# A two-direction state-space scan and the z projection beside it, issued in fixed rounds

## The reference, cut to what matters

```python
def ssd_chunked(xs, dt, a, bm, cm):            # one direction
    a_cs = jnp.cumsum(adt, axis=-1)
    decay_in = jnp.exp(jnp.where(tri, seg, -jnp.inf))        # 128 x 128 per chunk and head
    cb = jnp.einsum("bclgn,bcsgn->bcgls", cc, bc)            # 128 x 128 per chunk and group
    y_diag = jnp.einsum("bcgls,bcgrls,bcsgrp->bclgrp", cb, decay_in, xd)
    states = jnp.einsum("bclgn,bcgrl,bclgrp->bcgrpn", bc, decay_states, xd)
    h = h * dec + state                                      # over the chunks, in order
    y_off = jnp.einsum("bclgn,bcgrpn,bcgrl->bclgrp", cc, prev, jnp.exp(a_cs))
...
    y = y_fwd + y_bwd + d_skip * xs
    return rms_norm(y * jax.nn.silu(z), ssd_norm)            # z = h @ w_in[:, 768:1792]
```

## Time and profile before

| | |
|---|---|
| median of 3 runs | 2354.16 us (2347.55, 2354.16, 2356.76) |
| profiled execution | 2345.79 us, of which 2344.0 us are its span |
| PE busy | 2198.4 us, 94% |
| DVE, ACT, POOL busy | 1142.7, 1004.5, 962.0 us |
| granted PE clock, mean over the span | 0.961 |

### The profile page before, as it was taken

One profiled execution on the slowest core, in us unless ns is written; L12 is line 12 of the kernel. 1 busy time (PEld: TensorE's weight loads), 2 busy tenths in 40 slices (PEclk: granted clock), 3 DMA queues, 4 the chain that ended last, 5 costly groups with the idle time before them and its releaser, 6 DMA issues.

```text
span 2344.0 us, 28202 instructions
## 1 busy us (share of the span) xinstructions
PE 2198.4 (94%) x10837; PEld 1826.0 (78%) x10848; DVE 1142.7 (49%) x1836; ACT 1004.5 (43%) x2027; POOL 962.0 (41%) x730
## 2 busy tenths in 40 slices
PE   7999899999988997899999998998899999999997
PEld 5788778888877776778888877785697887888886
DVE  3445565554344666465554363664445335544322
ACT  5666444443235555244443254655243234323222
POOL 3655553433457652444333442224323334322232
PEclk9999999999999999799999997998899999999998
DMA  4111122232213221122222221110012232222221
GB/s 157 55 55 60 49 99 99 90 108 99 94 60 102 82 68 39 62 82 90 98 100 97 88 88 36 37 36 19 19 46 101 88 108 72 92 106 90 101 99 52
DMA packets 29846, 183.08 MB, mean 78 GB/s; under 512 B 3984, under 2 KB 4112, under 8 KB 11920
## 3 DMA queue, kind: packets, MB, share of 16 engines
q1 hardware_dynamic: 29712, 181.27, 22.4%
HBM read 174.97 MB, written 2.10 MB: 76 GB/s over the span
## 4 chain that ended last, share of the span: by engine, by line
PE 82%; DVE 6%; ACT 5%; issue 3%; POOL 2%; DMA 1%; SPq 0%; POOLq 0%; ACTq 0%; DVEq 0%
PE PS L1452 81%; PE PS L1577 1%; POOL LO L2735 1%; DVE bQS L2191 1%; PE PS L1690 0%; ACT HI L1779 0%; DMA RAW<-wall 0%; DVE aQS L2191 0%; DVE T_f L2263 0%; DVE XL L2268 0%; DVE YH L2293 0%; PE PS L1625 0%; POOL cQ L2818 0%; ACT bP L1995 0%; POOL cROT L2810 0%
## 5 line engine op out<-in xcount | busy, mean ns | idle before, releaser
L2735 POOL TENSOR_TENSOR LO<-RAW,HI 128x512 fp32r<-128x512 f32 (+2 forms) x382 | 540.9, 1432 | 601.6 <-ACT HI L1779 601.3
L1452 PE MATMUL PS<-XH,HI 128*128 128x512 f32 (+1 forms) x1584 | 637.6, 403 | 24.5 <-DVE XL L2191 6.7
L1452 PE MATMUL PS<-XH,LO 128*128 128x512 f32 (+1 forms) x1584 | 624.4, 394 | 0.0
L1452 PE MATMUL PS<-XL,HI 128*128 128x512 f32 (+1 forms) x1584 | 618.1, 395 | 1.0 <-DVE XL L2268 1.0
L1779 ACT ACTIVATE HI<-RAW 128x512 fp32r<-128x512 f32 (+3 forms) x668 | 365.4, 608 | 171.3 <-PE PS L1452 168.0
L2191 DVE TENSOR_TENSOR LO<-RAW,HI 128x512 fp32r<-128x512 f32 (+2 forms) x286 | 305.0, 1071 | 246.2 <-ACT HI L1779 245.8
L1452 PEld LDWEIGHTS PS<-XH,HI 128*128 128x128 f32 (+1 forms) x1584 | 302.2, 191 | 87.7 <-issue 20.4
L1452 PEld LDWEIGHTS PS<-XH,LO 128*128 128x128 f32 (+1 forms) x1584 | 301.4, 190 | 65.7 <-issue 0.8
L1452 PEld LDWEIGHTS PS<-XL,HI 128*128 128x128 f32 (+1 forms) x1584 | 300.8, 190 | 62.7 <-DVE XL L2268 2.5
L1452 PE MATMUL PS<-HH,HI 128*128 128x512 f32 x528 | 205.4, 389 | 0.0
L1452 PE MATMUL PS<-HL,HI 128*128 128x512 f32 x528 | 205.4, 389 | 0.0
(11 more groups left out here) (395 smaller groups left out, 3358.3 us busy)
## 6 DMA issues: line engine op xcount, KB each, us to landing
RAW<-wall SPq DMA_DIRECT2D x138, 1024.0 KB, 4.8
RAW<-wall SPq DMA_DIRECT2D x24, 896.0 KB, 4.4
bROT<-bTQ SPq DMA_DIRECT2D x64, 64.0 KB, 2.0
RAW<-wall SPq DMA_DIRECT2D x5, 512.0 KB, 3.3
XF<-xT SPq DMA_DIRECT2D x4, 512.0 KB, 5.2
outT<-XR SPq DMA_DIRECT2D x8, 256.0 KB, 2.0
FP<-cfp SPq DMA_DIRECT2D x1, 1024.0 KB, 6.7
MKF<-cmask SPq DMA_DIRECT2D x1, 704.0 KB, 10.8
```

What stands on the lines that cost most here:

```text
L1452: return e.matmul(out, a, b, start=start, stop=stop)
L2735: return e.tensor_tensor(out, x, h.bitcast(F32), ALU.subtract)
```

## The change

- The z units start right after the two CB products, and the generator `scan()` runs beside them at 1.12 steps per tick. It works in rounds: round r puts the exponent products of head r, the state product of item r-1, the state reading of item r-3, and y of head r-1, in that order on PE; `STATES` lists the state items, alternating directions. From round 2 on it waits until the last convolution is turned.
- Steps are split so that issue and completion stand apart: `se` (the exponentials), `sz` (the addition to Y), `sq` (scaling a reading and adding it), `sv` (taking a state in), `sd` (decaying the old state).
- The states alternate between two places (PRV and the new tiles PR2), so decaying doesn't wait for the reading.
- `em`: DVE adds the backward half of EM to the forward half and multiplies the sum with CB once. POOL has no part in it. `sy` has 4 products in place of 8, and there is one pair of banks for the exponents in place of two.
- z's gates go to tiles of their own (SZ, two units deep). Multiplying them into Y is a step `czm` of its own, put when the four heads of a group and all six state readings of its half are in Y. Unit i >= 2 waits for the `czm` of unit i-2.

```diff
-RATES = (0.37, 0.18, 1.12, 0.36, 1.0, 0.9, 0.9)
+STATES = ((0, 0, 0), (1, 0, 0), (0, 0, 1), (0, 1, 0), (1, 1, 0), (1, 0, 1), (0, 2, 0), (1, 2, 0), (0, 1, 1), (1, 1, 1), None,
+          (0, 2, 1), (1, 2, 1))
+RATES = (0.37, 0.18, 1.12, 1.12, 1.0, 0.9, 0.9)
...
+            while sdone[0] < 16 or sum(added) < 12:
+                while r >= 2 and ("cxt", CONV[-1]) not in steps:
                     yield
+                if 0 < r < 17:
+                    put("em", r - 1)
+                if item(r):
+                    put("sw", *item(r))
+                    if item(r)[1]:
+                        put("sd", *item(r))
+                if r < 16:
                     for dr in range(2):
+                        at_bank(("sh", r, dr), 2 + dr)
+                    put("sh", r)
                     yield
+                if item(r - 2):
+                    s = put("sv", *item(r - 2))
...
+                if item(r - 4):
+                    dr, idx, g = item(r - 4)
+                    freed[6] = ("sod", put("sq", dr, idx + 1, g))
+                    added[g] += 1
+                if item(r - 1):
+                    s = ("sp",) + item(r - 1)
+                    at_bank(s, 4 + s[1])
+                    put(*s)
                     yield
+                if r < 16:
+                    s = put("se", r)
...
+                if item(r - 3):
+                    dr, idx, g = item(r - 3)
+                    at_bank(put("so", dr, idx + 1, g), 6)
+                    yield
+                if 1 < r < 18:
+                    freed[7] = ("syd", put("sz", r - 2))
+                    sdone[0] = r - 1
+                if 0 < r < 17:
+                    at_bank(put("sy", r - 1), 7)
+                    yield
+                times()
...
-        first = opening()
-        while chores or together_chores:
-            chore()
-            next(first, None)
-        for _ in first:
-            pass
-        alongside(scans(), RATES[3])
-        until(lambda: sdone[0] >= 4 and all(finished))
+        alongside(scan(), RATES[3])
         for i in range(4):
             def evac(c, t):
-                if c == 0:
-                    until(lambda: sdone[0] >= 4 * i + 4)
-                return ("czd", put("cze", i, c, t))
+                if i >= 2:
+                    until(lambda: (i - 2, c) in timed)
+                s = put("cze", i, c, t)
+                gated.append((i, c))
+                times()
+                return "czd", s
...
                 for c in range(4):
-                    for dr in range(2):
-                        u = 1024 * (h % 2) + 512 * dr + 128 * c
-                        x = 1024 * c + 64 * h
-                        m = mm(PS[bank][:, 64 * c:64 * c + 64], EM[:, u:u + 128], XS[:, x:x + 64], dr == 0, dr == 1)
+                    u, x = 1024 * (h % 2) + 128 * c, 1024 * c + 64 * h
+                    m = mm(PS[bank][:, 64 * c:64 * c + 64], EM[:, u:u + 128], XS[:, x:x + 64])
...
-                e.wait_ge(SEM["sem"], when("sem", "sh", h)[1] - 1)
+                e.wait_ge(*when("sem", "se", h))
+                e.tensor_tensor(EM[:, u:u + 512], EM[:, u:u + 512], EM[:, u + 512:u + 1024], ALU.add).then_inc(SEM["smp"], 1)
+                e.wait_ge(*when("smp", *step))
                 e.tensor_tensor(EM[:, u:u + 512], EM[:, u:u + 512], blk(CB, h // 8), ALU.mult).then_inc(SEM["smd"], 1)
...
-            elif kind == "em":
-                h, = a
-                u = 1024 * (h % 2) + 512
-                e.wait_ge(*when("scbd", "cb", h // 8))
-                e.wait_ge(*when("sem", "sh", h))
-                e.tensor_tensor(EM[:, u:u + 512], EM[:, u:u + 512], blk(CB, h // 8), ALU.mult).then_inc(SEM["smp"], 1)
```

More of the change, by code:

```diff
@@ L1046, in second, with times @@
             xbc(j // 2)
-        sdone, finished, begun = [0], [False, False], set()
+        sdone, added, gated, timed = [0], [0, 0], [], []
+        def times():
+            for i, c in list(gated):
+                if sdone[0] >= 4 * i + 4 and added[i // 2] == 6:
+                    put("czm", i, c)
+                    gated.remove((i, c))
+                    timed.append((i, c))
         def c_times_b(g):
@@ L1055, in c_times_b @@
             freed[6] = ("scbd", s)
-        def head(h):
-            if h not in begun:
-                begun.add(h)
-                for dr in range(2):
[L1061 to L1091, removed]
-                    yield
[L1093 to L1098, removed]
-                        put(*s)
-                        freed[b] = ("sprv" if idx else "sprv0", s)
-                        if idx == 0:
-                            yield
-            finished[dr] = True
@@ L1105, in opening @@
-        def opening():
-            for h in range(2):
-                next(head(h))
-                yield
-                for _ in range(2 if h == 0 else 0):
-                    for dr in range(2):
-                        next(left[dr])
-                        yield
-                for n in range(4 * h, 4 * h + 4):
-                    put("y0", n)
-                next(products(h), None)
-                yield
-            for h in range(2):
-                next(sums(h), None)
-                yield
-                next(head(h + 2))
-                yield
-                next(products(h + 2), None)
-                yield
-            while ("cxt", 7) not in steps:
-                yield
-            for h in range(8, 16):
-                put("y0", h)
-                if h % 2:
-                    yield
-            for _ in range(2):
-                for dr in range(2):
-                    next(left[dr])
-                    yield
@@ L2139, in scalar @@
                 act(dst, src, ACT.Copy, scale=col("dskip", h)).then_inc(SEM["sy0"], 1)
-            elif kind == "sp" and a[1] == 0:
+            elif kind == "sv" and a[1] == 0:
                 dr, idx, g = a
-                e.wait_ge(*when("sst", *step))
-                act(blk(PRV, 2 * dr + g), PS[bank][:, :], ACT.Copy).then_inc(SEM["sprv0"], 1)
-            elif kind == "sh":
+                e.wait_ge(*when("sst", "sp", *a))
+                act(state(*a), PS[ag.bank_of[("sp",) + a]][:, :], ACT.Copy).then_inc(SEM["sprv0"], 1)
+            elif kind == "se":
                 h, = a
@@ L2828, in gpsimd @@
                 r = 32 * c + 16 * dr + 8 * g
-                if idx or g:
-                    e.wait_ge(*when("sst", "sp", dr, idx - (1 - g), 1 - g))
+                n = STATES.index(a)
+                before = [t for t in STATES[:n] if t and t[0] == dr]
+                if before:
+                    e.wait_ge(*when("sst", "sp", *before[-1]))
                 else:
```

127 lines of the change are left out of this document (78 added, 49 removed).

## The result

| | before | after |
|---|---|---|
| median (lowest to highest) | 2354.17 us (2347.55 to 2356.76) | 2328.73 us (2325.11 to 2332.43) |
| ratio, 95% interval | | 0.9904 [0.9874, 0.9934] |
| profiled execution, its span | 2345.79, 2344.0 us | 2325.11, 2323.3 us |
| the stage | 147.4 us | 119.6 us |

The forecast was 2325 us, and 118.5 for the stage. A second set of six runs of the changed kernel gave 2328.1 us and 0.991 [0.9893, 0.9928], with a stage of 119.6 again.

The account below looks back on a forecast made before the run. PE alone was taken to bound the z stretch. Work 108.0 + opening 3.7 + gates 3.3 + collisions 1.5 + hand-offs 2.0 = 118.5 us for 147.2, so 2354.2 - 28.7, say 2325 us; range 2311 to 2341.

Parts of the forecast that it names:

- PE work: PE's products in the stage: 121.8 us falls by 13.8 to 108.0, since y takes 4 products, not 8.
- The opening: Stage start: second head's exponents wait 1.0 us, last convolution piece 0.7, half clock costs 2.0; together 3.7 us.
- The gates: Rounds 10 and 11 lack column steps, 1.3 us; PE waits 2.0 behind eight gate multiplications on DVE; together 3.3 us.
- the sign that the prediction gave: PE idles longest before the reading that follows the eight gate multiplications, 2 us.
- Collisions and hand-offs: DVE and POOL working in the same tile cost PE 1.5 us; hand-offs in 16 rounds cost 2.0 us.
- The clock: Partly half clock for some 4 us at the stage's opening, then 1.00 from about 1608 us on.
- The surplus nearly all goes: Rival, chance 0.15: PE always finds work, waits and half clock come to 3 us; stage 111, total 2318 us.
- VectorE bound through GpSimd: Rival, chance 0.15: each POOL instruction stops DVE for its length, a round costs DVE 7.7 us; total 2336 us.
- The rule that the prediction cited: A DVE instruction with two SBUF inputs and a GpSimd one reading SBUF exclude each other for a whole instruction.
- The clock stays 0.83: Rival, chance 0.06: the scan stretch's clock of 0.83 holds over the whole stage; stage 138.6, total 2345.5 us.
- Rounds as one chain: Rival, chance 0.04: every head waits for the one before through all engines, 8.9 us per round; slower, 2364 us.

Follow-up runs that it names:

- experiment 1: Changed kernel without the sum of directions, y made with eight products as before: stage 130.6 us, median 2336.42 us, ratio to before 0.9934.
- experiment 11: The changed kernel run again, unaltered, beside versions made from it: 2328.1 us, ratio to before 0.991, stage 119.6 us.
- experiment 6: Changed kernel with the addition to Y first in its round and gate multiplications handed out one at a time: stage 115.0 us, median 2325.27 us, ratio to before 0.9898.
- Experiment 5: Changed kernel with the addition to Y moved first in its round, ahead of a z evacuation: stage 116.1 us, median 2322.38 us, ratio to before 0.9874.
- version 12: Changed kernel with addition to Y first, gates one at a time, room at second head and last y, sum on GpSimd: stage 110.0 us, 2318.71 us, ratio 0.9867.
- experiment 8: Changed kernel with the addition to Y first and EM's halves added twice on VectorE: stage 122.8 us, median 2331.48 us, ratio to before 0.9915.
- experiment 10: Changed kernel with addition to Y first, gates one at a time, and EM's halves added on GpSimd: stage 114.6 us, 2317.26 us, ratio to before 0.9861.
- experiment 2: Changed kernel with all rounds put before the first z unit: stage 130.2 us, median 2337.12 us, ratio to before 0.9936.
- Version 9: Changed kernel with addition to Y first, gates one at a time, more z steps before second head's exponents and last y: stage 115.8 us, 2319.61 us, ratio 0.9873.

## Why the prediction was right, step by step

It was right in the total and nearly so in the stage: 119.6 us for 118.5. By its terms:

- *PE work*: forecast 108.0, found 105.8. y at 0.90 us (forecast 0.92) holds, and experiment 1 shows the term with its sign turned. A state product or reading costs 0.86, not 0.93: I had priced them in the scan stretch, where each stands alone between waits; 24 of them were 1.7 us too dear.
- *The opening*: forecast 3.7, found 1.0. The wait for the first head's exponentials is 0.9 (forecast 1.0), the last convolution piece costs 0.07 (0.7), and the clock there was 1.00, not half (2.0). I took the half clock of the old opening over into the new one. In this execution it did not come; in the second one of the same kernel (experiment 11) 6.8 us of low clock began at 1607.3, just there. So that part of the term is neither right nor wrong: it varies.
- *The gates*: forecast 3.3, found 3.0 (0.5 and 0.6 in the dense rounds, 1.9 at the reading). The place and size are right, and so is the reason: with the eight multiplications handed out one at a time (experiment 6), the reading behind them does not wait. Against the sign that the prediction gave, it is not the longest idle time: that is 1.57 us before y at 1694.4, against 1.36 here.
- *Collisions and hand-offs*: forecast 1.5 + 2.0, found 6.4. This is the step that failed. I had reckoned VectorE's load and due times per round from what it must compute, 4.6 of 6.8 us, and did not walk the z evacuation through its queue. It is not late by work but stands ahead of the addition to Y and waits for a tanh. The two waits of which it is the plain cause, 1.0 and 1.6 us, are nearly the whole of what the term lacks. Experiment 5 takes both away, but brings others of 3 us, so that the sum of the waits falls by only 1.8. The collisions came about as forecast: products of 0.84 us and sums of 0.77, for 0.69 quiet, add 16 x 0.23 = 3.7 us to VectorE, and the two waits that stretched instructions cover, at 1621.05 and 1670.25, come to 1.4 us for the forecast's 1.5.
- *The clock*: forecast none behind the opening, found 6.8 us of low clock, 3.4 lost, after waits of 1.6 and 1.5 us before y at 1694.4 and 1709.4. Nothing in the sum stood for it, and no run here shows how to forecast it.

The errors are -2.2, -2.7, -0.3, +2.9 and +3.4, in sum +1.1: they cancel, and the close hit is partly luck.

The rivals. *The surplus nearly all goes* was out as to this kernel (13.8 us left, not 3), but it is what version 12 comes to: 4.2. *VectorE bound through GpSimd*: experiment 8 speaks against it (11 us more on VectorE brought 3.3 of waits), and experiment 10 puts the sum on GpSimd and loses nothing. But the collisions do reach PE in single places, as experiment 6 shows. The rule that the prediction cited, from the Trainium skill's "SBUF — State Buffer", section "Who interferes with whom", shows in single instructions of the timeline of after. Here the product in the last row takes 1.65 us for 0.69: GpSimd is through at 1620.10, and the product ends 0.56 us later. So the trace agrees with the rule. The mean of 0.84 is low because few of the products meet a GpSimd instruction: 13 of 16 take under 0.8 us and the others 1.41, 1.42 and 1.65.

```profile
1618.38 1.72 POOL L2729 TENSOR_TENSOR LO<-RAW,HI 128x512 fp32r<-128x512 f32 x1
1619.01 1.65 DVE L2640 TENSOR_TENSOR cEM<-cEM,cCB 128x512 f32<-128x512 f32 x1
```

*The clock stays 0.83*: it was 1.00 to 1680 and 0.92 after; in experiment 2, with z kept out, it was 0.86 in the scan. *Rounds as one chain* did not come: from the first head's exponents at 1604.9 to the last y at 1709.4 us lie sixteen rounds, 6.5 us each.

What the change is worth by its halves, in stage lengths: the sum with its four products 20.1 us in the old order and 11.0 in the new; all the rest (z beside the scan, the rounds, the split steps, the second place) 16.8 without the sum and 7.7 with it. Part of this is the clock: without what it took (15.4 us before, 6.9 with the sum alone, 5.1 with the rest alone, 3.4 in after) the first is worth 11.5 and 9.3 and the second 6.5 and 4.3. They are worth less together than one by one, as they would be if both eat from the same surplus. The prediction added them as if they were apart, and this held because it took only the y work for the first. What z beside the scan is worth by itself is experiment 2 against after: 10.6 us, nearly all of it low clock.

Of the 27.8 us the stage gained, the medians show 25.4 and the two profiled executions 20.7. The part ahead of the stage took 4.3 us more and the part behind it 2.8 more, in the same instructions, inside the 13 and 4 us by which they vary here.

## What to carry to other kernels

When steps of two streams are woven into one in-order queue, walk each queue at the places where an instruction of the one waits for its own stream's next input: what stands behind it is late although its engine is idle. Put what frees a bank for the bounding engine ahead of it, then look at what now stands behind that: here six waits of 5.9 us lost their cause and the sum of waits fell by 1.8. Side work can go to the engine with the slack although it is slower there (GpSimd at 1.36 us for VectorE's 0.77): the waits fell, and no time was lost. Price a stage as work, half clock and waits apart, because a version can lose its waits and show no gain where the clock happened to be low.

## What was not expected of the hardware

- The low clock did not simply follow the waits. Version 9 had 3.2 us of waits and 13.7 us of low clock, version 5 8.6 and 3.4. In after a wait of 1.4 us at 1685.6 left the clock at full, and one of 1.57 us at 1694.4 was followed by the lower level at 1697.2. The changed kernel's two profiled executions had 6.8 us of it each, once at 1607 and once in two pieces at 1697 and 1711. What decides it in one execution stays open, and with it up to 7 us of any stage here.
- The part ahead of the stage, 1600 us of identical instructions, had between 109 and 146 us at the lower clock in the fourteen profiled executions.
